# The third up weights' parts ahead of the second gate's copy and read-out in the paired bodies of a gated feed-forward stage

## The reference, as far as it matters

```python
def convffn(h, hist, w_gate, w_up, conv_w, conv_b, w_down):
    gconv, new_hist = causal_dwconv(h @ w_gate, hist, conv_w)
    return (jax.nn.silu(gconv + conv_b) * (h @ w_up)) @ w_down, new_hist
```

## Time and profile before

| | before |
|---|---|
| median of 3 runs | 1180.44 us (1179.88 to 1180.45) |
| the profiled execution's own time | 1180.11 us |
| its span, first to last instruction | 1178.0 us |
| TensorE busy | 1169.3 us, 99% |
| VectorE busy | 850.6 us, 72% |
| ScalarE busy | 594.4 us, 50% |
| mean granted TensorE clock | 1.000 |

### The profile page before, as it was taken

One profiled execution on the slowest core, in us unless ns is written; L12 is line 12 of the kernel. 1 busy time (PEld: TensorE's weight loads), 2 busy tenths in 40 slices (PEclk: granted clock), 3 DMA queues, 4 the chain that ended last, 5 costly groups with the idle time before them and its releaser, 6 DMA issues.

```text
span 1178.0 us, 25284 instructions
## 1 busy us (share of the span) xinstructions
PE 1169.3 (99%) x10438; PEld 1127.2 (96%) x10438; DVE 850.6 (72%) x1462; ACT 594.4 (50%) x1088; POOL 21.1 (2%) x50
## 2 busy tenths in 40 slices
PE   9999999999999999999999999999999999999998
PEld 8999999999999999999999999999999999999998
DVE  7766676889898764445686776868798888876443
ACT  6333346565655543335456565556766565562221
POOL 0000000000000000000000000000000000000000
PEclk9999999999999999999999999999999999999999
DMA  8455535675545454454567766659544645546541
GB/s 221 134 162 154 177 113 156 192 206 168 153 152 160 154 171 146 147 183 151 171 207 197 218 172 190 201 150 252 147 144 150 190 145 171 158 131 187 136 118 40
DMA packets 285943, 193.67 MB, mean 164 GB/s; under 512 B 40433, under 2 KB 282153, under 8 KB 284678
## 3 DMA queue, kind: packets, MB, share of 16 engines
q1 hardware_dynamic: 282636, 137.04, 43.0%
q0 software_dynamic: 1792, 54.43, 12.5%
q10 hardware_dynamic: 1402, 0.61, 0.2%
HBM read 184.52 MB, written 64.16 MB: 211 GB/s over the span
## 4 chain that ended last, share of the span: by engine, by line
PE 88%; DVE 7%; ACT 2%; issue 2%; DMA 1%; SPq 0%; DVEq 0%; ACTq 0%
PE acc L2361 17%; PE acc L2379 16%; PE acc L2383 8%; PE acc L2380 8%; PE acc L2381 8%; PE acc L2382 8%; PE M L2562 7%; PE N L2562 5%; PE acc L2417 3%; DVE wl L1520 1%; PE N L2348 1%; PE N L2709 1%; PE M L2417 1%; DVE u L2158 1%; PE M L2348 1%
## 5 line engine op out<-in xcount | busy, mean ns | idle before, releaser
L1007 ACT ACTIVATE wh<-wraw 128x1024 fp32r<-128x1024 f32 (+1 forms) x147 | 150.8, 1026 | 251.1 <-PE acc L2383 148.4
L1520 DVE TENSOR_TENSOR wl<-wraw,wh 128x1024 fp32r<-128x1024 f32 (+1 forms) x147 | 174.5, 1187 | 83.3 <-ACT wh L1007 74.8
L2379 PE MATMUL acc<-h_both,wh 128*128 128x512 f32 x576 | 218.8, 380 | 1.4 <-DVE wl L1520 1.0
L2361 PE MATMUL acc<-h_both,wh 128*128 128x256 f32 (+2 forms) x1152 | 178.1, 277 | 0.6 <-DVEq L2092 0.5
L2383 PE MATMUL acc<-h_both,wl 128*128 128x264 f32 x576 | 160.2, 278 | 0.0
L2380 PE MATMUL acc<-h_both,wh 128*128 128x264 f32 x576 | 159.1, 276 | 0.0
L2381 PE MATMUL acc<-h_both,wh 128*128 128x264 f32 x576 | 159.1, 276 | 0.0
L2382 PE MATMUL acc<-h_both,wl 128*128 128x256 f32 x576 | 157.1, 273 | 0.0
L2361 PEld LDWEIGHTS acc<-h_both,wh 128*128 128x128 f32 x1152 | 152.1, 191 | 1.9 <-DVEq L2092 1.3
L2379 PE MATMUL acc<-y_both,wh 128*128 128x512 f32 x356 | 135.3, 380 | 0.0
L2381 PEld LDWEIGHTS acc<-h_both,wh 128*128 128x128 f32 x576 | 108.9, 189 | 15.3
(11 more groups left out here) (351 smaller groups left out, 2535.8 us busy)
## 6 DMA issues: line engine op xcount, KB each, us to landing
out_dram<-in_cache_kv_d_dram POOLq DMA_DIRECT2D x24, 1364.0 KB, 6.4
wraw<-in_ffn_w_gate_dram SPq DMA_DIRECT2D x44, 512.0 KB, 4.2
wraw<-in_attn_w_qkv_dram SPq DMA_DIRECT2D x36, 512.0 KB, 3.9
out_dram<-in_cache_kv_d_dram POOLq DMA_DIRECT2D x8, 2044.0 KB, 8.3
wraw<-in_ffn_w_up_dram SPq DMA_DIRECT2D x28, 512.0 KB, 5.7
wraw<-in_ffn_w_down_dram SPq DMA_DIRECT2D x32, 448.0 KB, 3.7
wraw<-in_sc_w_in_dram SPq DMA_DIRECT2D x23, 512.0 KB, 3.8
big<-in_ffn_w_up_dram SPq DMA_DIRECT2D x16, 512.0 KB, 7.0
```

The costliest lines, as they stand in the source:

```text
L1007: nc.scalar.activation(wh[c % 2][:, 0:k], wraw[:, c % 4, 0:k], ACT.Copy).then_inc(hi_done, 1)
L1520: V.tensor_tensor(wl[c % 2][:, 0:k], wraw[:, c % 4, 0:k], wh[c % 2][:, 0:k].bitcast(F32), ALU.subtract).then_inc(split_done, 1)
L2361: ins = T.matmul(pair_bank(dst, b, cut), w[c % 2][:, k, :], paired(a[:, k0 + k], b, cut), start=(first and k == 0 and n == 0), stop=(last ...
L2379: T.matmul(wide, h[:, k, :], wide_pairs(both[:, :, k0 + k]), start=start, stop=False)
```

## The change

On ScalarE, in a paired body, the copy of the second gate (`keep_gate`) goes behind the high part of chunk 4 and behind the copy to `C1[:, 0]` with its two waits; on VectorE the low part of chunk 4 goes ahead of the second gate's read-out. Nothing is added or removed.

```diff
@@ -1218,11 +1218,11 @@
                     unit_hi(it, 3, gu.chunk(it, 0))
                     conv(f)
                     silu(f)
-                    keep_gate(it, 1, 1, acc[:, 1])
                     unit_hi(it, 4, gu.chunk(it, 1))
                     act.wait_ge(part_done, j + 1)
                     act.wait_ge(y_ready, f + y0)
                     keep_part(C1[:, 0], M[:, 0])
+                    keep_gate(it, 1, 1, acc[:, 1])
                     conv(f + 1)
                     unit_hi(it, 5, gu.chunk(it, 2))
                     act.wait_ge(part_done, j + 2)
@@ -1919,9 +1919,9 @@
                     dve.wait_ge(sums_ready, 3 * i + 2)
                     V.tensor_tensor(a21, a12, s2, ALU.subtract).then_inc(sums_ready, 1)
                     conv(f)
+                    unit_lo(it, 4)
                     dve.wait_ge(chunk_used, gu.chunk(it, 1) + 1)
                     wide_gate_out(f + 1, acc[:, 1], n + 2)
-                    unit_lo(it, 4)
                     dve.wait_ge(snap, 4 * i + 1)
                     dve.wait_ge(chunk_used, gu.chunk(it, 2) + 1)
                     V.tensor_tensor(C1[:, 0], M[:, 1, 0:HALF], C1[:, 0], ALU.add)
```

## The result

| | before | after |
|---|---|---|
| median | 1180.12 us (1179.65 to 1180.45, 7 runs) | 1184.03 us (1183.80 to 1184.71, 7 runs) |
| ratio, with its 95% interval | | 1.0034 [1.0022, 1.0045] |
| the profiled execution's own time, span | 1180.11 us, 1178.0 us | 1184.01 us, 1181.9 us |

The change makes the kernel 3.9 us slower, where 4.5 us was forecast. The granted clock is 1.000 in both. The page of after gives the same instructions. TensorE is busy 2.9 us longer than in the earlier trace rows and idle only 1.0 us longer (1181.9 - 1172.2 = 9.7 against 8.7), though it does the same work: a matmul's end is modelled, and a wait shorter than what is left of the matmul ahead is counted as busy. So the page alone hides most of the loss.

What follows compares the result with a forecast made beforehand. TensorE, busy 1169.3 of 1178.0 us, was taken as the bound. Layer 0's 0.87 + 0.11 + 1.25 = 2.23 and layer 1's 0.88 + 0.11 + 1.25 = 2.24 gave +4.5 on 1180.1: 1184.6 us, range 1182.0 to 1187.2.

Steps and rivals of the forecast that it cites:

- The round: Bodies 3 to 8: the VectorE-ScalarE loop takes 20.27 us against TensorE's 20.02, 0.25 us lost per body.
- Rival 3: Middle bodies: wakes of 0.14 us throughout make the round longer, 20.5 us, total 1187.3 us; chance 12%.
- The step named as the costly one: Middle body: VectorE idles 1.83 us for chunk 4's high part instead of 1.17 us for the gate's copy.
- The first paired bodies: First paired body of each layer: late `C2[:, 1]` copy stalls TensorE 0.87 us, and 1.30 less 0.42 gained, 0.88.
- signs of 0.9 and 1.3: After trace, first paired bodies: TensorE waits for ScalarE's snapshot of N some 0.9 and 1.3 us.
- The other part of the gain: Layer 1's first paired body: an earlier low part of chunk 4 saves TensorE 0.16 us at block e.
- Body 3: Body 3 of each layer: the next chunk 0's low part lets TensorE go on at 270.31, due 270.20; 0.11 us lost.
- The sum: Whole kernel: layer 0 loses 2.23 us, layer 1 2.24, together +4.5 us on 1180.1.
- Rival 1: Middle bodies lose nothing and only the first paired bodies stall, 0.87 + 0.88 = 1.8 us: 1181.9 us; chance 15%.
- Rival 2: Not slower: the 0.42 us gain stays and nothing stalls at `C2[:, 1]` in the first paired body, 1179.7 us; chance 5%.
- rival 4: The move does nothing, as chunk 4's high part is ready long before VectorE asks: 1180.1 us; chance 3%.
- The joints of VectorE's queue: Low part to read-out: the skill's drain rule would add 0.09 us a body, 1185.6 us; the row adds nothing.

Runs made afterwards that it cites:

- the `y` split moved: Against the full change: in bodies 3 to 8 `y_high` moved ahead of the first gate's copy, `y_low` ahead of chunk 4's low part; 1181.81 us.
- the first of the two idle-time kernels: Against before, first paired bodies only: chunk 4's high part and `C1[:, 0]` copy ahead of SiLU, low part ahead of read-out, `C2[:, 1]` copy earlier; 1179.42 us.
- the second experiment: The full change made in all paired bodies but each layer's first, against the kernel before; 1182.07 us, ratio 1.0016.

## Why the prediction was right, step by step

**The round** was summed as 7.75 + 7.27 + 0.61 + 4.64 = 20.27 us and is 7.74 + 7.27 + 0.60 + 4.63 = 20.24. Each term holds to 0.01, so the wakes were taken right: the high part released the low part within 0.04 us of its end (ScalarE's row is 342.75 + 1.04 = 343.79, VectorE starts at 343.83) and not 0.14 behind, as the copy of the gate did. Rival 3 (20.5 us) falls with it. But three terms that are each 0.01 too long make 0.03 us, and over ten bodies that is the first part of the difference between 4.5 and 3.9: 10 x (0.25 - 0.22) = 0.3 us. This is the term that was mis-sized.

**The step named as the costly one** is the one that costs. VectorE's idle time ahead of the low part was given as 1.83 us and is 1.75 (the prediction's own times for the two ends, 340.12 and 341.86, are 1.74 apart; the 1.83 was counted from 340.03); the read-out starts 344.97 - 342.08 = 2.89 us after the taps of f, forecast 2.88, where it was 1.17. Against block a it starts at 3.30 us instead of 1.26; 0.32 of these 2.04 us are not the step itself but VectorE's whole chain, which runs later against TensorE once the reserve is gone (the taps end 0.41 us after block a instead of 0.09).

**The first paired bodies:** forecast 0.87 and 0.88 us, measured 0.86 and 0.92; the brackets say 0.60 and 1.03 us where the text gave signs of 0.9 and 1.3. The signs named what TensorE loses, and a bracket counts from the last matmul's shown end: its 0.28 us less the usual distance of 0.11 is lost too, and 0.10 for the restart (0.49 instead of 0.39). That makes 0.60 + 0.27 = 0.87 and 1.03 + 0.27 = 1.30. In layer 1 a gain stands against it. TensorE still waits for the snapshot of M, but less than in the earlier trace rows:

```profile
890.48 0.49 PE L2562 MATMUL M<-h_sums,wh 128*128 128x260 f32 x2 [0.39 <-ACT sv L1207]
```

0.66 - 0.39 = 0.27 us against the forecast's 0.26. The other part of the gain, for the low part of chunk 4, was put at 0.16; what is left for it is 1.30 - 0.92 - 0.27 = 0.11. That wait is too short for a bracket, but before has its mark, at block e:

```profile
890.37 0.49 PE L2562 MATMUL N<-h_sums,wh 128*128 128x260 f32 x2
```

It starts 0.12 us behind the matmul ahead of it, one hundredth more than usual, and lasts 0.49 instead of 0.39. After has 0.39 there. Body 3: 0.08 and 0.09, forecast 0.11.

**The sum.** By the traces, layer 0 pays 2.04 us and layer 1 2.10, together 4.14; forecast 2.23 and 2.24. The spans differ by 3.9 (the first block a starts 0.04 late). The remaining -0.24 us lies between the layers, in a place that the prediction didn't look at. VectorE's key product in the output projection waits for a DMA in before's execution and not in after's:

```profile
794.09 1.23 DVE L2151 TENSOR_TENSOR skv<-skv 128x1024 f32<-128x1024 f32 x1 [0.27 <-DMA skv<-new_rows]
```

```profile
795.85 1.22 DVE L2151 TENSOR_TENSOR skv<-skv 128x1024 f32<-128x1024 f32 x1
```

The same wait is 0.51 us with ScalarE's half alone, 0.24 with the first body alone, 0.29 with the `y` split moved, 0.79 with the first of the two idle-time kernels, and absent in the other four. The time from block a of body 9 in layer 0 to that of body 2 in layer 1, less this wait, is 503.73 to 503.77 us in seven of the ten traces, before and after among them (504.01 - 0.27 = 503.74 and 503.76), so the wait does pass on to TensorE. It isn't ordered by how late the stage begins, so it is taken to vary from one execution to the next; no run repeats one kernel's trace, so that isn't shown. It makes every comparison of two traces here uncertain by some tenths of a us.

**Rivals.** Rival 1, only the first bodies stall, falls by the second experiment. Rival 2 falls by the stalls and rival 4 by the row at 344.97.

**The joints of VectorE's queue.** The new pair, low part and then read-out, starts at 343.83 and 344.97: 1.14 us for an operation of 1.23, as in the pair of the earlier trace rows. The rule of the Trainium skill (VectorE: DVE Perf Modes, "The DRAIN you can't avoid"), that the next operation waits until the pipe has emptied, would have set 0.09 us more here; the row doesn't show it. The same section of the Trainium skill adds that a next operation which isn't held starts earlier, which the prediction left out; both pairs start like that. The sum rests on the row alone.

## What to carry to other kernels

When two in-order engines hand work back and forth, sum the chain once around, from one event to the same event in the next body, with its idle times, and compare it with the bound engine's period: here 19.3 against 20.02 us meant free and 20.24 meant not, while the busy shares of VectorE and ScalarE over 20 us of after (86% and 55%, both lower than before) said nothing. An idle gap ahead of a step is only a reserve if what the step waits for doesn't move with it: putting a step that waits for a 1.04 us copy ahead of one that waits for a 0.36 us copy lengthened the round though no work was added. Look also at the first body of a loop by itself, where the engines stand differently to each other than in the steady state.

## What the runs showed of the hardware beyond the expected

The same two engines wake each other at different prices. In the rows read here ScalarE's high part released VectorE 0.04 us after its shown end (343.79 to 343.83), the convolution start too (346.22 + 0.83 = 347.05 to 347.09), the gate's copy 0.13 us after (with ScalarE's half alone, 344.93 + 0.38 = 345.31 to 345.44). The prediction had left open whether 0.14 would hold throughout, which was worth 2.7 us; it does not. What makes the gate's copy dearer, its length, what it reads or what its reader reads, wasn't tried.
